# The index weights as eight extra columns of the index-key tile, in a two-block transformer kernel

## What is computed

```python
proj = h @ w_in                                   # 512 x 1024 times 1024 x (2048+128+512+64+8)
q, lat, qi, ki, wi = jnp.split(proj, [o1, o2, o3, o4], axis=-1)
qi = qi.reshape(B, S, IDX_HEADS, IDX_DIM)         # 8 heads of 64
wi = wi.astype(jnp.float32) * (IDX_HEADS ** -0.5) # one weight per token and head: 512 x 8
isc = jax.nn.relu(jnp.einsum('bqhd,bsd->bqhs', qib, ki))
isc = jnp.einsum('bqhs,bqh->bqs', isc, wib)       # weighted sum over the 8 heads
_, sel = lax.top_k(isc, topk)                     # 128 keys for each query
```

## Time and profile before

| | us |
|---|---|
| median of three runs | 2167.24 |
| the profiled execution's own time | 2167.39 |
| its span, first to last instruction | 2165.6 |
| TensorE busy (matmul) | 2034.1 |
| GpSimd busy | 1215.7 |
| VectorE busy | 1034.0 |
| ScalarE busy | 603.3 |

### The profile page before, as it was taken

The page is one execution under the profiler, slowest core; times in us unless marked ns, Lnnn a source line. Parts: engine busy times, 40 slices in busy tenths (PEclk is TensorE's granted clock), DMA queues, the critical chain, the costliest instruction groups (busy, mean ns, idle before and its releaser), DMA issues.

```text
span 2165.6 us, 26887 instructions
## 1 busy us (share of the span) xinstructions
PE 2034.1 (94%) x9346; PEld 1624.7 (75%) x9346; DVE 1034.0 (48%) x1611; ACT 603.3 (28%) x1134; POOL 1215.7 (56%) x678
## 2 busy tenths in 40 slices
PE   5999799997998899899899999999999998999999
PEld 4876678886887677666788888878686577888887
DVE  4456469989225800365443333131784744333422
ACT  2226210000113320597231111121316823111210
POOL 6650568886663766433566666654352046666664
PEclk9999889999998899999999999988999999999999
DMA  6330258887231222100423333321121012333331
GB/s 232 127 117 1 78 172 287 287 286 248 87 97 49 78 97 92 45 1 0 156 78 97 97 97 93 95 84 49 60 77 40 1 55 73 97 97 97 97 97 68
DMA packets 62327, 221.15 MB, mean 102 GB/s; under 512 B 6913, under 2 KB 7169, under 8 KB 62129
## 3 DMA queue, kind: packets, MB, share of 16 engines
q1 hardware_dynamic: 44928, 161.25, 23.4%
q10 hardware_dynamic: 17328, 58.95, 7.7%
HBM read 218.03 MB, written 2.14 MB: 102 GB/s over the span
## 4 chain that ended last, share of the span: by engine, by line
PE 62%; ACT 6%; DVE 6%; issue 2%; DMA 0%; POOL 0%; ACTq 0%; DVEq 0%
PE bank L280 17%; PE bank L281 17%; PE bank L282 17%; PE bank L310 1%; PE bank L315 1%; PE bank L311 1%; PE bank L588 1%; ACT y L658 1%; ACT L666 1%; PE bank L381 1%; PE bank L450 1%; PE bank L475 1%; DVE big L1530 1%; ACT tmp L515 1%; ACT tmp L521 1%
## 5 line engine op out<-in xcount | busy, mean ns | idle before, releaser
L280 PE MATMUL bank<-a_hi,w_hi 128*128 128x512 f32 x2072 | 813.3, 393 | 10.3 <-DVE a_lo L812 4.9
L282 PE MATMUL bank<-a_hi,w_lo 128*128 128x512 f32 x2072 | 808.5, 390 | 0.0
L281 PE MATMUL bank<-a_lo,w_hi 128*128 128x512 f32 x2072 | 808.5, 390 | 0.0
L857 POOL TENSOR_SCALAR w_hi<-raw 128x1024 fp32r<-128x1024 f32 x299 | 356.9, 1194 | 755.7 <-PE bank L282 496.0
L859 POOL TENSOR_TENSOR w_lo<-raw,w_hi 128x1024 fp32r<-128x1024 f32 x299 | 764.9, 2558 | 24.9
L280 PEld LDWEIGHTS bank<-a_hi,w_hi 128*128 128x128 f32 x2072 | 390.4, 188 | 94.1 <-POOL w_lo L859 5.5
L282 PEld LDWEIGHTS bank<-a_hi,w_lo 128*128 128x128 f32 x2072 | 390.3, 188 | 81.9
L281 PEld LDWEIGHTS bank<-a_lo,w_hi 128*128 128x128 f32 x2072 | 390.5, 188 | 81.2 <-issue 0.7
L1334 DVE CUSTOM_DVE_ANT_0 y<-y,cond 128x1024 f32<-128x1024 f32 x96 | 212.7, 2267 | 0.5 <-DMA y<-in_ada 0.5
L1345 DVE SCALAR_TENSOR_TENSOR tmp<-bank,vecs,tmp 128x511 f32<-128x511 f32 x88 | 66.0, 750 | 263.1 <-ACT tmp L1093 263.1
L1093 ACT ACTIVATE tmp<-bank,vecs 128x512 f32<-128x512 f32 x88 | 68.5, 781 | 372.2 <-PE bank L282 364.6
(11 more groups left out here) (207 smaller groups left out, 2307.2 us busy)
## 6 DMA issues: line engine op xcount, KB each, us to landing
raw<-in_stream SPq DMA_DIRECT2D x299, 512.0 KB, 3.5
y<-in_ada ACTq DMA_DIRECT2D x96, 512.0 KB, 4.7
x<-in_x SPq DMA_DIRECT2D x4, 512.0 KB, 7.1
bias<-in_bias ACTq DMA_DIRECT2D x1, 2048.0 KB, 14.1
y<-rel_rows ACTq DMA_DIRECT2D x1, 2048.0 KB, 9.4
bias<-rel_rows ACTq DMA_DIRECT2D x1, 2048.0 KB, 14.2
out<-x SPq DMA_DIRECT2D x8, 256.0 KB, 2.1
cond<-in_c ACTq DMA_DIRECT2D x1, 512.0 KB, 9.2
```

The source lines that it names most:

```text
L280: pe.matmul(o, lhs_hi, rhs_hi, start=start, stop=False, **kw)
L281: pe.matmul(o, lhs_hi, rhs_lo, start=False, stop=False, **kw)
L282: return pe.matmul(o, lhs_lo, rhs_hi, start=False, stop=stop, **kw)
L857: pool.tensor_scalar(w_hi[:, s, :], raw[:, j, :], 1.0, 1.0, ALU.mult, ALU.mult).then_inc(high_ready, 1)
```

## The change

The 8 index-weight columns are put into the `ki` block, in place of the first 8 columns of the key's second copy. (The columns behind them still hold the rest of that copy, and nobody reads them.) The tile `ki` then gives the key in partitions 0 to 63 and the weights in partitions 64 to 71, head by token. ScalarE copies these 8 rows to `index_rows`, which lies in the unused half of `squares`, and writes the key's upper copy from bank partitions 0 to 63 to `tmp` partitions 64 to 127. TensorE turns the 8 rows into token-major form by four transposes, behind the `lat` tile, into bank 4, and ScalarE scales them into `wi`. The separate input, its load, its split and the 96 matmuls are dropped. The `lat` tile no longer waits for all banks and goes to bank 1 in place of bank 0; the `dq` tiles move one bank along too.

```diff
@@ TensorE
-            pe.wait_ge(wi_split, 2)
-            for t in range(TT):
-                for k in range(DC):
-                    m = pe_three_passes(pe, bank[7][:, t * 8:(t + 1) * 8], a_hi[:, k, t * P:(t + 1) * P],
-                                        a_lo[:, k, t * P:(t + 1) * P], wi_hi[:, k, :], wi_lo[:, k, :], k == 0, k == DC - 1)
-            m.then_inc(wi_ready, 1)
...
                 if n == 0:
                     pe.wait_ge(*freed("ki", 1))
                     pe.wait_ge(index_init, 8)
+                    pe.wait_ge(wi_taken, 1)
...
-            pe_begin(pe, "lat")
-            pe_tile(pe, "lat", 0, 0)
+            pe_tile(pe, "lat", 0, 0, first_bank=1)
+
+            pe.wait_ge(wi_rows, 1)
+            for t in range(TT):
+                m = pe.transpose(bank[4][:, t * IDX_HEADS:(t + 1) * IDX_HEADS], index_rows[:, t * P:(t + 1) * P],
+                                 ident[IDX_DIM:IDX_DIM + IDX_HEADS, IDX_DIM:IDX_DIM + IDX_HEADS])
+            m.then_inc(wi_ready, 1)
             for i in range(D_HEADS):
 
-                pe_tile(pe, "dq", i % 4, i, first_bank=1)
+                pe_tile(pe, "dq", i % 4, i, first_bank=2)
@@ ScalarE
-            a.dma_start(wi_raw[:], wi_in).then_inc(wi_landed, 16)
...
             a.wait_ge(block_done, START["ki"] + 1)
             a.activation(tmp[0:64, 2, :], bank[0][0:64, :], ACT.Copy)
-            a.activation(tmp[64:P, 3, :], bank[0][64:P, :], ACT.Copy).then_inc(banks_free["act"], 1)
-            a.wait_ge(wi_ready, 1)
-            a.activation(wi[:].rearrange("p t h -> p (t h)"), bank[7][:, 0:TT * IDX_HEADS], ACT.Copy,
-                         scale=IDX_HEADS ** -0.5).then_inc(wi_taken, 1)
+            a.activation(index_rows, bank[0][IDX_DIM:IDX_DIM + IDX_HEADS, :], ACT.Copy).then_inc(wi_rows, 1)
+            a.activation(tmp[64:P, 3, :], bank[0][0:64, :], ACT.Copy).then_inc(banks_free["act"], 1)
...
             head_square(0)
+            a.wait_ge(wi_ready, 1)
+            a.activation(wi[:].rearrange("p t h -> p (t h)"), bank[4][:, 0:TT * IDX_HEADS], ACT.Copy,
+                         scale=IDX_HEADS ** -0.5).then_inc(wi_taken, 1)
@@ VectorE
-            v.wait_ge(wi_landed, 16)
-            v.tensor_copy(wi_hi[:].rearrange("p k h -> p (k h)"), wi_raw[:]).then_inc(wi_split, 1)
-            v.wait_ge(wi_split, 1)
-            v.tensor_tensor(wi_lo[:].rearrange("p k h -> p (k h)"), wi_raw[:], f32(wi_hi[:]).rearrange("p k h -> p (k h)"),
-                            ALU.subtract).then_inc(wi_split, 1)
+            v.wait_ge(*low_done("mix1", DC - 2))
@@ weights
-        "ki": tile_blocks(np.concatenate([ki, ki], axis=1))
+        "ki": tile_blocks(np.concatenate([ki, dsa[:, o4:], ki[:, IDX_HEADS:]], axis=1))
```

More of the change, by code:

```diff
@@ L127, with two_blocks @@
 CONSTS = ["ident", "ones", "neg_ones", "neg_suffix", "upper", "causal", "strict"]
-def two_blocks(nc, x_in, p_in, vecs_in, stream_in, ada_in, consts_in, bias_in, onehot_in, rel_in, wi_in,
+def two_blocks(nc, x_in, p_in, vecs_in, stream_in, ada_in, consts_in, bias_in, onehot_in, rel_in,
                sgu_g_in, sgu_b_in, bs_in, ws_in, c_in, scratch, out):
@@ L172, in two_blocks @@
         z_rstd = sb("z_rstd", [P, 16])
-        wi_raw = sb("wi_raw", [P, DC * IDX_HEADS])
-        wi_hi = sb("wi_hi", [P, DC, IDX_HEADS], F32R)
-        wi_lo = sb("wi_lo", [P, DC, IDX_HEADS], F32R)
         wi = sb("wi", [P, TT, IDX_HEADS])
@@ L232, in two_blocks @@
         x_landed = [sem(f"x_landed{j}") for j in range(X_PARTS)]
-        rows_landed, cond_landed, p_landed, wi_landed = sem("rows_landed"), sem("cond_landed"), sem("p_landed"), sem("wi_landed")
+        rows_landed, cond_landed, p_landed = sem("rows_landed"), sem("cond_landed"), sem("p_landed")
         onehot_landed = sem("onehot_landed")
@@ L250, in two_blocks @@
         out_stored = sem("out_stored")
-        wi_split, wi_ready, wi_taken = sem("wi_split"), sem("wi_ready"), sem("wi_taken")
+        wi_rows, wi_ready, wi_taken = sem("wi_rows"), sem("wi_ready"), sem("wi_taken")
         relu_ready, index_ready, index_added = sem("relu_ready"), sem("index_ready"), sem("index_added")
@@ L432, in two_blocks @@
         d_sems, d_units = attention("d", D_HEADS)
+        index_rows = squares[IDX_DIM:IDX_DIM + IDX_HEADS, 1, :]
         head_sums = bank[7][:, TT * IDX_HEADS:TT * IDX_HEADS + (D_HEADS + 1) * TT]
@@ L1273, in head_square @@
                     a.wait_ge(qsum_ready, m - 1)
-                a.activation(tmp[:, m % 2, :], bank[m % 4][:], ACT.Square).then_inc(qsq_ready, 1)
+                a.activation(tmp[:, m % 2, :], bank[(m + 1) % 4][:], ACT.Square).then_inc(qsq_ready, 1)
                 if m == 0:
-                    a.activation(lat_hi[:], bank[0][:], ACT.Copy).then_inc(lat_split, 1)
-                a.activation(k_lat[:] if m == 0 else big[:, m - 1, :], bank[m % 4][:], ACT.Copy).then_inc(banks_free["act"], 1)
+                    a.activation(lat_hi[:], bank[1][:], ACT.Copy).then_inc(lat_split, 1)
+                a.activation(k_lat[:] if m == 0 else big[:, m - 1, :], bank[(m + 1) % 4][:], ACT.Copy).then_inc(banks_free["act"], 1)
             def index_relu(n):
@@ L1654, in weight_stream @@
         "gu2": pair_blocks(a["ffn_w_up_2"][0]), "down2": a["ffn_w_down_2"][0].reshape(FC, P, D),
-        "qi": tile_blocks(dsa[:, o2:o3]), "ki": tile_blocks(np.concatenate([ki, ki], axis=1)), "lat": tile_blocks(dsa[:, o1:o2]),
+        "qi": tile_blocks(dsa[:, o2:o3]), "ki": tile_blocks(np.concatenate([ki, dsa[:, o4:], ki[:, IDX_HEADS:]], axis=1)), "lat": tile_blocks(dsa[:, o1:o2]),
         "dq": tile_blocks(dsa[:, 0:o1]), "uv": a["dsa_w_uv_2"][0].transpose(1, 0, 2).reshape(1, P, BLOCK),
@@ L1680 @@
     a = {k: np.asarray(v) for k, v in inputs.items()}
-    wi = a["dsa_w_in_2"][0][:, -IDX_HEADS:]
     arrays = {
@@ L1691 @@
         "rel": a["rel_bias_2"],
-        "wi": wi.reshape(DC, P, IDX_HEADS).transpose(1, 0, 2).reshape(P, DC * IDX_HEADS),
         "sgu_g": a["sgu_ln_g"][0],
```

## The result

The changed kernel took 2154.2 us (median of four runs) where the kernel before took 2168.0, ratio 0.9940 (95% interval 0.9923 to 0.9957). Timed again with the experiments it took 2151.8 us (median of six) against 2169.4, ratio 0.9931 (0.9917 to 0.9945). So it is 0.6 to 0.7% faster. The forecast was 2150.8 us, 16.6 us less; the two pairs of medians say 13.7 and 17.6.

The account below looks back on a forecast made before the run. TensorE, busy 94% of the span, was taken to bound the kernel. 2167.39 - 15.52 (small matmuls) - 1.72 (`lat` at half clock) + 0.6 (transposes) = 2150.75, forecast 2150.8 us, range 2147.5 to 2154.5.

Parts of the forecast that it names:

- The 96 matmuls and `lat` at half clock, 15.52 + 1.72: Between `ki` and `dq` 0 on TensorE: dropping the small matmuls saves 15.52 us, `lat` at full clock another 1.72.
- Four transposes, 0.6: On TensorE between `lat` and `dq` 0: the added transposes cost 0.6 us, with ends 0.4 and 1.5.
- The covers: ScalarE's copied rows and scaled copy finish before they are needed, with 4 and 5 us to spare, costing nothing.
- What is late next: From the first head sum on, every engine starts from TensorE and pause ends move together, so the whole gain passes on.
- The range: Whole-kernel time 2147.5 to 2154.5 us, allowing for three runs spanning 3.5 us and (b) at both sides.
- (a): At the removed matmuls: the slow clock was not their doing, 13.6 us at 1.2 GHz stay; 2157.2 us, chance 0.03.
- (b): Index stage: VectorE's chain meets GpSimd otherwise, two more or fewer long operations; 2155 or 2147 us, chance 0.05.
- (c): The stage is set by VectorE anyway and TensorE only waits longer: no change, 2167.4 us, chance 0.02.
- (d): The transposes bring the clock down before the `dq` tiles: slower, 2228 us if all 16 ran so, chance 0.01.

Follow-up runs that it names:

- long run of 96: The changed kernel with its four transposes made 24 times over, 96 in place of 4: ki's first copy to first head sum 21.5 us against 11.3.
- without the pause: The changed kernel with index scores spread over 11 dq tiles in place of 6, and `ki` not waiting for all banks: median 2144.8 us.
- second profile: Profile of the changed kernel, unchanged, when timed again with the experiments: median 2151.8 us of six runs.
- first profile: Profile of the changed kernel's slowest execution among its first four: 2157.86 us.

## Why the prediction was right or wrong

*The 96 matmuls and `lat` at half clock, 15.52 + 1.72.* Right. The stage from `ki` to the first head sum lost 16.65 us where the terms with the transposes said 16.64, in both profiles of the changed kernel and in that with the load kept.

*Four transposes, 0.6.* Right in sum: 0.44 from `lat`'s end (24 x 0.227 behind 1494.18) to `dq` 0 at 1500.06, and `dq` 0 took 5.59 in place of 5.44. The estimate beside it from the Trainium skill (TensorE: Matmul & The Clock Gate, the section on LDWEIGHTS), 0.107 us for each of the four, came near by chance: in the long run of 96 one takes 0.062 us at full clock. Four of those are 0.25 us; the rest of the 0.59 stands at the change to short matmuls and back, for which I had allowed 0.14.

*The covers.* Right. The rows were copied at 1495.6, TensorE asked at 1499.6, and without cover the wait costs 1.3 us. The scaled copy ended at 1501.5, 5 us before its first use. The load at the start was worth nothing that shows (2152.2 with it, 2151.8 without).

*"What is late next": "the whole gain should pass on".* This step failed, by 1.57 us. I had the pauses of TensorE at the index scores in front of me and argued that both their ends move together. They did, but a pause has a second price, the clock behind it, and whether it is paid changed though the pause did not: no in the one profile of the kernel before but yes in both its variants with small matmuls between, yes in all five profiles with `lat` in bank 1 and the scores in six tiles, no with `lat` in bank 0, where all comes 2.2 us later, and no without the pause. I had looked for a loss of clock at what was added and not at what was moved. The 16.65 us were there at the first head sum, and 16.65 - 1.57 = 15.1 of them at the last. That is the change's own worth, ratio 0.9930, which is where the second comparison lies (0.9931). The runs show that one and the same pause costs 1.57 us or nothing, by what went before it. That what counts is the time at which it comes fits them, but no run moved that time alone, and the cause stays open.

*The range.* The start to A took from 1481.4 to 1494.4 us over the profiles of kernels that are nearly alike up to there, 13 us, nearly as much as the change is worth. I had taken 3.5 us for it from three runs; in 13 later runs the kernel before spread over 10 us (2162.7 to 2172.6). With four and six runs the two medians of the changed kernel lie 2.4 us apart, and the first of them 3.4 us above the forecast: about 1.6 us of that is the failed step, the rest is this spread.

*Rivals.* (a) was wrong as put: with the small matmuls gone the clock stays. But they need not stand back to back for it to fall: one 512-column matmul before every four did not prevent it. (b) did not happen: VectorE's long operations of the stage are the same five (2.24 us at the first, 2.25 before). Such a meeting did change the time elsewhere, by 2.9 us near 540 us, between two runs. (c) fell: VectorE's 20.5 us of waiting is unchanged. (d) fell for four transposes, and 96 do bring the clock down.

## What to carry to other kernels

A handful of output columns can cost TensorE as much as three full tiles (17.24 us here against 5.44 for one) if the activations are the stationary operand: 96 weight loads, each for 8 columns. Put such columns into the unused ones of a tile that is computed anyway and turn the small result round. Price short matmuls twice: for themselves and for the clock, which fell under them here even at 100% busy. After moving work, look again at every pause behind it, since its price in clock can change while its length does not.

## What the runs showed of the hardware

The clock fell to 0.50 under 8-column matmuls with a 512-column one before every four (0.67 us for the five) and stayed at 1.00 with one to one (0.34 us for the pair). A transpose of 8x128 took 0.062 us at full clock and about 0.10 at half; a matmul of 128 loaded columns by 8 moved ones took 0.11 and 0.21. ScalarE copied 8 partitions x 512 in the same 0.59 us as 64, and from partitions 0 to 63 to 64 to 127 at no extra cost. VectorE's four operations on `gains`, 8 elements a partition each, took 2.42 us together beside a GpSimd split and 0.40 ahead of it. And programs that are nearly alike differed by 13 us in the first 1480 us, with different half-clock stretches at pauses of the same length: the pause of 2.15 us near 54 us was followed by full clock in the kernel before and the second profile, and by half clock in the first profile.
